# The modulation product turned round: the activations stand in the array, the fp32 weights stream past them

## The reference

```python
mod_l = (jax.nn.silu(c) @ w_mod[i] + b_mod[i]).reshape(b, N_MOD, 1, D_MODEL)
mod_c = (jax.nn.silu(c_ctx) @ w_mod[i] + b_mod[i]).reshape(N_MOD, 1, D_MODEL)
x_lat = x_lat + 0.5 * mod_l[:, 2] * swiglu(modulate(x_lat, norm_gain[i, 0], mod_l[:, 0], mod_l[:, 1]),
                                           ffn_a_in[i], ffn_a_out[i])
...
```

## Time and profile before

| what | value |
|---|---|
| median of 3 runs | 2542.73 us (2538.7, 2542.73, 2543.7) |
| span of the profiled execution | 2538.7 us |
| time of the profiled execution | 2538.7 us: the lowest of the three runs, equal to its span to the tenth |
| PE busy | 2444.8 us, 96% |
| DVE busy | 1424.4 us, 56% |
| ACT busy | 1100.3 us, 43% |
| DMA, mean | 151 GB/s |
| `in_w_mod` loads | 72 of 1024 KB, 8.3 us from issue to landing (median) |

### The profile page before, as it was taken

One profiled execution on the slowest core, in us unless ns is written; L12 is line 12 of the kernel. 1 busy time (PEld: TensorE's weight loads), 2 busy tenths in 40 slices (PEclk: granted clock), 3 DMA queues, 4 the chain that ended last, 5 costly groups with the idle time before them and its releaser, 6 DMA issues.

```text
span 2538.7 us, 44873 instructions
## 1 busy us (share of the span) xinstructions
PE 2444.8 (96%) x17697; PEld 1591.1 (63%) x17697; DVE 1424.4 (56%) x2006; ACT 1100.3 (43%) x1604; POOL 261.0 (10%) x255
## 2 busy tenths in 40 slices
PE   6999999998999999999999899999999999999998
PEld 3444444464544444444444468878888888878887
DVE  7557443468475552365532444357766765786774
ACT  6445323245354442354433321255545555565553
POOL 1125001005100000100003101021101000010001
PEclk8999999999999999999999999999999999999999
DMA  9897532330246654355544243226886675554674
GB/s 311 180 192 234 168 108 75 91 100 17 83 143 189 198 163 114 109 179 179 180 135 114 67 124 93 67 83 179 236 245 179 200 222 150 154 142 121 193 206 131
DMA packets 658235, 384.17 MB, mean 151 GB/s; under 512 B 11179, under 2 KB 654608, under 8 KB 657992
## 3 DMA queue, kind: packets, MB, share of 16 engines
q1 hardware_dynamic: 653432, 369.27, 49.8%
q0 software_dynamic: 4112, 11.44, 3.0%
q10 hardware_dynamic: 576, 1.83, 0.2%
HBM read 381.41 MB, written 1.08 MB: 151 GB/s over the span
## 4 chain that ended last, share of the span: by engine, by line
PE 87%; DVE 9%; ACT 2%; issue 1%; DMA 1%; ACTq 0%; SPq 0%; DVEq 0%
PE PS L651 24%; PE PS L653 24%; PE PS L652 24%; DVE WL L1615 2%; PE PS L668 2%; PE PS L670 2%; PE PS L669 2%; DVE arena L1851 1%; PE PS L1011 1%; DVE XL L1857 1%; PE PS L611 1%; PE PS L612 1%; ACT WH L1140 1%; PE PS L977 1%; ACT arena L1140 1%
## 5 line engine op out<-in xcount | busy, mean ns | idle before, releaser
L651 PE MATMUL PS<-XH,WH 128*128 128x512 f16 (+2 forms) x2912 | 943.5, 324 | 19.5 <-DVE XL L1857 14.0
L652 PE MATMUL PS<-XL,WH 128*128 128x512 f16 (+2 forms) x2912 | 943.1, 324 | 0.0
L653 PE MATMUL PS<-XH,WL 128*128 128x512 f16 (+2 forms) x2912 | 942.4, 324 | 0.0
L1140 ACT ACTIVATE WH<-W 128x1024 f16<-128x1024 f32 (+1 forms) x520 | 557.5, 1108 | 684.4 <-PE PS L653 593.1
L1615 DVE SCALAR_TENSOR_TENSOR WL<-W,WH 128x1024 f16<-128x1024 f32 (+1 forms) x520 | 669.1, 1317 | 248.5 <-ACT WH L1140 248.3
L651 PEld LDWEIGHTS PS<-XH,WH 128*128 128x128 f16 x2912 | 286.3, 98 | 204.0 <-issue 17.2
L653 PEld LDWEIGHTS PS<-XH,WL 128*128 128x128 f16 x2912 | 286.6, 98 | 180.2 <-issue 4.4
L652 PEld LDWEIGHTS PS<-XL,WH 128*128 128x128 f16 x2912 | 286.3, 98 | 170.1 <-issue 3.7
L651 PE MATMUL PS<-arena,WH 128*128 128x256 f16 (+1 forms) x1184 | 379.3, 320 | 1.4 <-DVE WL L1615 1.4
L653 PE MATMUL PS<-arena,WL 128*128 128x256 f16 (+1 forms) x1184 | 379.2, 320 | 0.0
L652 PE MATMUL PS<-arena,WH 128*128 128x256 f16 (+1 forms) x1184 | 379.2, 320 | 0.0
(11 more groups left out here) (286 smaller groups left out, 2273.8 us busy)
## 6 DMA issues: line engine op xcount, KB each, us to landing
arena<-in_w_mod SPq DMA_DIRECT2D x72, 1024.0 KB, 8.3
W<-in_ffn_a_in SPq DMA_DIRECT2D x88, 512.0 KB, 5.0
W<-in_ffn_b_in SPq DMA_DIRECT2D x88, 512.0 KB, 4.7
W<-in_w_ffn_gu SPq DMA_DIRECT2D x88, 512.0 KB, 4.3
W<-in_ret_in SPq DMA_DIRECT2D x48, 512.0 KB, 4.4
W<-in_ffn_a_out SPq DMA_DIRECT2D x32, 704.0 KB, 5.9
W<-in_ffn_b_out SPq DMA_DIRECT2D x32, 704.0 KB, 5.9
W<-in_w_ffn_down SPq DMA_DIRECT2D x32, 704.0 KB, 5.8
```

The costliest lines, as they stand in the source:

```text
L651: mm(dst, wh, xh, start=(kp == 0 and c == 0), stop=False, skip_group_check=True)
L652: mm(dst, wh, xl, start=False, stop=False, skip_group_check=True)
L653: return mm(dst, wl, xh, start=False, stop=(kp == g["parts"] - 1 and c == kc - 1), skip_group_check=True)
L1140: return act.activation(dst, src, ACT.Copy, scale=scale)
```

## The change

`w_mod` is now cut in 36 strips of 512 columns, each loaded as two halves of 512 rows (1 MB, rows of 2 KB). The stationary operand is `silu_w`: 32 columns, of which two hold silu(c) and silu(c_ctx) and 30 are zero. The fp32 weights stream past it in pieces of 128 columns, each of the four pieces of a strip on a column group of its own. A half strip is 4 chunks x 4 groups = 16 fp32 matmuls (`pe_mod`). The result lies on partitions 32j and 32j+1 with the modulation index along the row; ACT copies it to SBUF (`mod_copy`), one fp32 matmul with the copy as its 128x128 stationary and 8 columns of the unit matrix turns it (`pe_mod_turn`), and DVE copies that to `modT` (`mod_drain`). The split instructions of `w_mod` on ACT and DVE and their fp16 buffers are gone. SP's load of a half now waits for PE (`mod_used`) where it waited for the split.

```diff
-        M32 = [area(19968 + 2048 * k, DC, 2 * P) for k in range(2)]
+        M32 = [area(19968 + 2048 * k, DC // 2, 4 * P) for k in range(2)]
...
@@ sync: mod_load
-                    sp.wait_ge(mod_lo, 2 * (m0 + k - 2) + 2 + 4 * i)
-                src = mod_w[:, layer, :, bass.ds(256 * (first + k) + 512 * i, 2 * P)]
+                    sp.wait_ge(mod_used, m0 + k - 1 + 2 * i)
+                src = mod_w[:, layer, 4 * k:4 * k + 4, bass.ds(256 * first + 512 * i, 4 * P)]
                 sp.dma_start(M32[k], src).then_inc(mod_loaded[k], 16)
@@ tensor
-            def pe_mod(m, k, wh=MWH, wl=MWL, slot=None):
...
-                    for c in range(DC):
-                        mm(dst, wh[slot][:, t, c], silu_s[:, c, :], start=(c == 0), stop=False, skip_group_check=True)
-                        ins = mm(dst[:, 0:2], wl[slot][:, t, c], silu_s[:, c, 0:2], start=False, stop=(c == DC - 1),
-                                 skip_group_check=True)
+            def pe_mod(strip, k):
...
+                    pe.wait_ge(mod_loaded[k], 16 * (strip - STRIPS_FIRST))
+                if k == 0 and not (isinstance(strip, int) and strip < 1):
+                    pe.wait_ge(mod_copied, strip)
+                for c in range(DC // 2):
+                    for j in range(4):
+                        ins = mm(PS[32 * j:32 * j + 32, 6, 0:P], silu_w[:, 4 * k + c, :], src[:, c, P * j:P * j + P],
+                                 start=(k == 0 and c == 0), stop=(k == 1 and c == DC // 2 - 1), skip_group_check=True)
                 ins.then_inc(mod_used, 1)
+
+            def pe_mod_turn(strip):
+
+                pe.wait_ge(mod_copied, strip + 1)
+                if not (isinstance(strip, int) and strip < 1):
+                    pe.wait_ge(mod_drained, strip)
+                heads = eye.rearrange("p (j n) -> p j n", j=4)[:, :, 0:2]
+                mm(PS[:, 7, 0:8].rearrange("p (j s) -> p j s", j=4), mod_row[:, :], heads, start=True, stop=True, skip_group_check=True)\
+                    .then_inc(mod_turned, 1)
...
                         if first and g["w0"] == 0:
-                            for m in range(MOD_FIRST + 2 * b, MOD_FIRST + 2 * b + 2):
-                                pe_mod(m, m % 2)
+                            if b == 1:
+                                pe_mod_turn(STRIPS_FIRST)
+                            for k in range(2):
+                                pe_mod(STRIPS_FIRST + b, k)
                         elif mods:
-                            pe_mod(g["m0"] + b + 2 * i, b)
+                            if b == 0 and not first:
+                                pe_mod_turn(g["m0"] // 2 - 1 + i)
+                            pe_mod(g["m0"] // 2 + i, b)
...
@@ scalar
+            def mod_copy(strip):
+
+                act.wait_ge(mod_used, 2 * strip + 2)
+                if not (isinstance(strip, int) and strip < 1):
+                    act.wait_ge(mod_turned, strip)
+                copy(mod_row[:, :], PS[:, 6, 0:P]).then_inc(mod_copied, 1)
...
+                def turn_of(i, mods):
+                    for k in range(2):
...
+                    if mods:
+                        mod_copy(g["m0"] // 2 - 1 + i)
...
+            act_root(0)
+            for strip in range(STRIPS_FIRST):
+                mod_copy(strip)
             begin(GEMMS[0], (0,))
@@ vector
+            def mod_drain(strip):
+
+                dve.wait_ge(mod_turned, strip + 1)
+                dve.tensor_copy(modT[:, bass.ds(4 * strip, 4), :], PS[:, 7, 0:8].rearrange("p (j s) -> p j s", j=4)).then_inc(mod_drained, 1)
...
-                            ins = stt(m, m, 1.0 / W_SCALE, pcol[:, at + a:at + b], ALU.mult, ALU.add)
+                            ins = tt(m, m, pcol[:, at + a:at + b], ALU.add)
...
-            mod_finish(MOD_FIRST, 32, [(0, 1), (0, 2)], [(0, 2)], [(0, 5)])
-            run("ffn_0a_out", between={b: lambda n=b - 2: filter_step(n) for b in range(2, 7)})
+            run("ffn_0a_out", between={2: lambda: (finish("ffn_0a_in", MOD_FIRST, 32, [(0, 1), (0, 2)], [(0, 2)], [(0, 5)]), filter_step(0))}
+                | {b: lambda n=b - 2: filter_step(n) for b in range(3, 7)})
```

More of the change, by code:

```diff
@@ L741, in pe_gemm @@
                     begin = mods
+                if mods and begin < n:
+                    turn_of(begin, False)
+                    pe_mod_turn(g["m0"] // 2 + mods - 1)
+                    begin += 1
                 if begin < n:
@@ L841, in keep_on @@
                     mm(PS[:, 3, 0:SEQ], ones, mats[:, 0:2, :].rearrange("p a b -> p (a b)"), start=True, stop=True, skip_group_check=True)
-            for m in range(MOD_FIRST):
-                pe_mod(m, m % 2, MWH_first, MWL_first, m % 4)
-                if m >= 3:
+            for strip in range(STRIPS_FIRST):
+                pe_mod(strip, 0)
+                if strip:
                     keep_on(1)
-                if m == 2:
+                pe_mod(strip, 1)
+                if strip == 0:
                     pe_spread(0)
+                else:
+                    keep_on(1)
+                pe_mod_turn(strip)
             pe.wait_ge(rel_loaded, 48)
@@ L1213, in act_gemm @@
                     return
[L1215 to L1231, removed]
+                def turn_of(i, mods):
+                    for k in range(2):
+                        if g["late"] is not None and is_ffn:
+                            split(g, i, k, tiles=(0,))
+                            silu(i - 1, k)
+                            split(g, i, k, tiles=(1,))
+                            hidden(i - 1, k)
+                            continue
+                        if is_ffn:
+                            silu(i - 1, k)
+                        split(g, i, k)
+                        if is_ffn:
+                            hidden(i - 1, k)
+                    if mods:
+                        mod_copy(g["m0"] // 2 - 1 + i)
+                start = 1
+                if g["mods"]:
+                    with act.Fori(1, g["mods"]) as i:
+                        turn_of(i, True)
+                    start = g["mods"]
+                    if start < n:
+                        turn_of(start, True)
+                        start += 1
+                if start < n:
+                    with act.Fori(start, n) as i:
+                        turn_of(i, False)
                 for k in range(2):
@@ L1334, in _ @@
             squares(0, range(DC))
-            mod_first_split(0)
             act.wait_ge(pcol_ready, 1)
+            act.wait_ge(silu_clear, 1)
             for s, name in enumerate(("c", "c_ctx")):
                 at = COL[(name, None)]
[L1339 to L1345, removed]
+                act.activation(silu_w[:, :, s], pcol[:, at:at + DC], ACT.Silu).then_inc(silu_ready, 1)
+            act_root(0)
+            for strip in range(STRIPS_FIRST):
+                mod_copy(strip)
             begin(GEMMS[0], (0,))
@@ L1752, in dve_gemm, with turn_of @@
                 elif g["kind"] == "ffn":
-                    for lo, hi, mods in ((1, g["mods"], True), (max(g["mods"], 1), n, False)):
-                        if lo < hi:
-                            with dve.Fori(lo, hi) as i:
-                                for k in range(2):
-                                    product(i - 1, k)
-                                    split(g, i, k)
-                                    rest(i - 1, k)
-                                    if mods:
-                                        mod_drain(g["m0"], i - 1, k)
-                                        mod_split(g["m0"], i, k)
+                    def turn_of(i, strip):
+                        for k in range(2):
+                            product(i - 1, k)
+                            split(g, i, k)
+                            rest(i - 1, k)
+                        if strip is not None:
+                            mod_drain(strip)
+                    start, strip0 = 1, g["m0"] // 2
+                    if g["mods"]:
+                        turn_of(1, STRIPS_FIRST if w0 == 0 else None)
+                        with dve.Fori(2, g["mods"]) as i:
+                            turn_of(i, strip0 - 2 + i)
+                        start = g["mods"]
+                        if start < n:
+                            for i in range(start, n):
+                                turn_of(i, strip0 - 2 + i if i < start + 2 else None)
+                            start = n
+                    if start < n:
+                        with dve.Fori(start, n) as i:
+                            turn_of(i, None)
                     for k in range(2):
@@ L2039, in _ @@
             run("ffn_0b_in")
-            mod_finish(32, 54, [(1, 0)], [(0, 8), (1, 2)], [])
-            run("ffn_0b_out", between={3: lg_step})
+            run("ffn_0b_out", between={2: lambda: finish("ffn_0b_in", 32, 54, [(1, 0)], [(0, 8), (1, 2)], []), 3: lg_step})
             run("ffn_1a_in")
```

125 lines of the change are left out of this document (35 added, 90 removed).

## The result

The changed kernel takes 2553.23 us (median of 16, 2549.69 to 2555.15), the kernel before 2542.54 in the same session (16, 2538.53 to 2550.28): ratio 1.0039, 95% interval 1.0030 to 1.0049. The profiled executions span 2552.8 and 2538.7 us: +14.1, where +14.8 was forecast. The forecast of 2557 is 3.8 above the median and in its range. That the sum came out so well is luck: four terms were off by 2 to 3 us each, in both directions. This is what most of the experiments are about.

A forecast was written before the change was run, and what follows sets the result against it. PE was taken to bound the loops, DVE the first 67 us. Terms, chiefly +17.4 for halves and +4.6 for turns less gains at the start, sum to +14.8: 2553.5, plus 4.0 for the median, about 2557 (2546 to 2570).

The forecast's parts named there:

- The half strip: PE in the loops: a half strip takes 1.10 us against 0.80 for the old piece, 58 x 0.30 = +17.4 us.
- The turn: PE ahead of a loop turn's first half: the turning matmul adds 0.14 us; all turns together +4.6 us.
- The jump: PE where the loop jumps back: longer instructions let the sequencer run ahead, regaining 2.0 us of 4.8.
- The start: Up to norm 0's `dve_apply`: no splits on DVE gains 2.3 us, 2 KB load rows 0.7, together -3.0.
- Behind block 0: PE after block 0: the new product takes 1.95 us where splitting pieces 8 and 9 took 3.58, -1.6 us.
- block 1 with its product: Block 1 of `ffn_0a_in` regains 1.7 us by running at full clock; the product after it costs +0.5.
- The new wait in `ffn_0a_in`: SP's half-strip loads now wait for PE's use of the buffer and may come late: +1.0 us (0 to 6).
- Nothing else moves on the path: Rest of the kernel: last strips' drain and `mod_finish` and POOL's waits for `mod_used` add no time.
- the hidden shape changes (1): Loops: array shape changes hide behind fp16 matmuls, a half costs only its 0.85 us body; 2536 us, chance 0.10.
- the fourfold speed (3): Product on PE: swapping operands and tiling columns cuts it to a quarter of its 0.80 us; 2500 us, chance 0.02.
- the serial groups (4): Product on PE: four column groups with different streams do not run side by side, 3.4 us a half; 2710, chance 0.02.
- the falling DMA queue (2): `ffn_0a_in`: turns 2 to 6 each wait some 2 us for `mod_copy` or a split; 2567 us, chance 0.12.

The follow-up runs named there:

- whole strip: Changed kernel with both half strips of a turn placed together behind the second block, the turn ahead of them: 2547.07 us, ratio 1.0013.
- quarter: Changed kernel issuing only one of four 128-row pieces per half from strip 5 on, the rest of the product left out: 2518.81 us, ratio 0.9903.
- full width: Changed kernel with the product from strip 5 on replaced by four fp32 matmuls a half over all 128 stationary columns: 2542.77 us, ratio 1.0004.
- the other pair of runs: Changed kernel, and the same with its ten first w_mod loads each issued as two, in 1 KB rows: the latter 2552.14 us, ratio 1.0045.
- paced: Changed kernel with GpSimd's eight groups of bias loads released every second block instead of every block: 2548.76 us, ratio 1.0032.

## Why the prediction was right

- *The half strip, +0.30.* Right: 1.11 us against 0.81. Entry 0.09, body 0.85, slow first set and leaving 0.16, each as read from the earlier trace rows; of the predicted 0.25 of entry, first set and leaving, whole strip, quarter and full width gave 0.24, 0.24 and, without 0.04 for leaving fp32, 0.21. The Trainium skill (TensorEngine Tiling (Array Packing), Key Properties) has the drain at a change of tiling mode. These runs agree in that each change costs time, 0.24 us in and out; that it is a drain they can't show. The same page of the Trainium skill, Performance Considerations, would have the swap pay, and here it doesn't, since 0.81 us for 32 small fp16 matmuls was no more than the fp32 body alone.
- *The turn, 0.14.* 0.13. Behind fp16 work alone it is 0.22.
- *The jump, -2.0.* Mis-sized: none of it is seen any more, 28 x 0.15 = -4.2.
- *The start, -3.0.* Mis-sized, -6.0. The part that DVE's chain gave up, 2.3, held; the loads, for which I allowed 0.7, came 3.6 us earlier, 1.7 by their rows (1.1 by the other pair of runs) and 1.9 by a landing place that the change moved unasked. By its own sign, `dve_apply` from 43.5 to 44.2, this step was wrong: it began at 40.51.
- *Behind block 0 -1.6, block 1 with its product -1.2.* Both right to 0.1.
- *The new wait in `ffn_0a_in`, +1.0.* Mis-sized: 4.1 in this execution, within the bounds of 0 to 6. The cause is the one named, the bias loads' traffic. The step leaned on a misread number: 8.3 us is not what the longest load takes but the median of the w_mod loads. In the kernel before, loads issued beside the bias loads already took up to 21.8 us, and up to 9.1 behind them; and the 162 GB/s of the earlier trace rows are those of one stretch, from 90 to 190 us it was 180 to 199. The sign of PE without waits in the loops failed by this one wait. In the kernel with rows of 1 KB, whose loops are the same, the wait is absent, so its size changes from one execution to the next.
- *"Nothing else moves on the path."* Failed: +2.1 in norms 1 to 4, as the clock fell in three of them before the spreading matmuls were through. Why it falls earlier there stays open.

The missed terms are -3.0, -2.2, +3.1 and +2.1 and cancel to nothing. The median also came in 1.6 below its own profiled execution, where the forecast had taken it 4.0 above. The mechanism on PE was right; that the sum came within 1 us of the trace was not earned. The sign was safe without these terms, since 17 us in the loops stood against at most 9 at the start. Of the rivals, the hidden shape changes (1), the fourfold speed (3) and the serial groups (4) are refuted by the half's 1.11 us; the falling DMA queue (2) came in one turn out of ten in this execution.

## What to carry to other kernels

Price a small product on TensorE by what it does to its neighbours: if it needs another column shape than the large ones around it, each visit costs 0.24 us here, with 4, 16 or 32 matmuls in it, so batch the visits or keep the shape. A rewrite can be worth it in the stage where the vector engines lead and cost in the stage where TensorE does; look whether the two stages can have different forms. And when a sum comes out right, go through it term by term.

## What the runs showed of the hardware

- The same first loads move at 341, 369 to 376 and 393 GB/s, by rows of 1 or 2 KB and by where they land: an area at byte 112128 of the partition (a multiple of 512) was faster than one at 111232 or 112192 (128 and 64 bytes off it).
- Sixteen fp32 matmuls of 128 columns on four column groups take 0.85 us (32 records of 26.5 ns), as long as four of them over the full width.
- A hardware loop's jump on TensorE costs 0.15 us behind 64 short fp16 instructions (32 matmuls and their 32 weight loads); behind a half strip in fp32 none is seen (1.01 us with it, 1.02 without).
- Weight loads of the hardware queue took up to 22.5 us to land beside the unpaced bias loads of short rows, at most 11.8 us beside paced ones, and up to 9.5 us when issued behind them (loads of 0.5 and 1 MB, 80 to 320 us).
- The granted clock falls from 1.00 to 0.50 around the norms' waits, before or after the same eight matmuls, which take 0.88 or up to 1.66 us. All 12 norms in the three profiles of the kernel before had the short form; why is open.
